# Last merge and output units of a two-block model on GpSimd's queue, five experts' units ahead of them, lower parts moved between sums

## The reference

```
h = rms_norm(x) * (1 + sc_m) + sh_m
proj = h @ w_in                                   # split into 9 parts, the last are 3 x 1024 gates
branches = [rglru(...), diff_attention(...), swa_attention(...)]
merged = sum_n sigmoid(gate_n) * (branch_n @ w_branch[n])      # 512 x 1024 each
x = x + g_m * (merged @ w_out)                                 # 1024 x 1024
h = rms_norm(x) * (1 + sc_f) + sh_f
top 4 of 32 experts per token by h @ w_router; softmax weights
x = x + g_f * sum over the four of  act(h @ w1[e] + b1[e]) @ w2[e] + b2[e]
```

## Time and profile before

| | |
|---|---|
| median of 3 runs | 2604.34 us (2603.31 to 2606.9) |
| profiled execution | 2605.9 us |
| its span in the trace | 2604.0 us |
| TensorE busy | 2567.9 us (99% of the span) |
| VectorE, ScalarE, GpSimd busy | 1350.1, 783.2, 73.6 us |
| TensorE's granted clock | 1.00 in every window used here |
| moved by DMA | 705.42 MB |

### The profile page before, as it was taken

The page is one execution under the profiler, slowest core; times in us unless marked ns, Lnnn a source line. Parts: engine busy times, 40 slices in busy tenths (PEclk is TensorE's granted clock), DMA queues, the critical chain, the costliest instruction groups (busy, mean ns, idle before and its releaser), DMA issues.

```text
span 2604.0 us, 39752 instructions
## 1 busy us (share of the span) xinstructions
PE 2567.9 (99%) x16005; PEld 1896.9 (73%) x16005; DVE 1350.1 (52%) x1781; ACT 783.2 (30%) x1318; POOL 73.6 (3%) x95
## 2 busy tenths in 40 slices
PE   9999999999999999999999999999999999999998
PEld 9989898999999899999999988833333333333333
DVE  6866785687688668657863684312112122112112
ACT  4414441443244144423433363122121121121111
POOL 0010200000000110000001000000000000000000
PEclk9999999999999999999999999999999999999999
DMA  6685443456655853344563634899999999999999
GB/s 231 212 287 178 139 146 146 151 179 227 219 180 184 303 172 125 135 146 162 178 219 109 230 125 175 322 416 426 427 427 427 428 427 427 427 427 428 427 428 411
DMA packets 265644, 705.42 MB, mean 271 GB/s; under 512 B 13108, under 2 KB 155392, under 8 KB 215744
## 3 DMA queue, kind: packets, MB, share of 16 engines
q1 hardware_dynamic: 253504, 663.66, 66.2%
q0 software_dynamic: 9856, 36.41, 3.9%
q10 hardware_dynamic: 2176, 3.83, 0.5%
HBM read 699.61 MB, written 6.60 MB: 271 GB/s over the span
## 4 chain that ended last, share of the span: by engine, by line
PE 79%; DMA 8%; SPq 8%; DVE 2%; ACT 1%; issue 1%; DVEq 0%; ACTq 0%; POOLq 0%
PE acc L1922 11%; PE acc L1124 6%; PE mix L1128 6%; PE acc L1126 6%; PE acc L1937 5%; PE acc L1197 5%; SPq L951 4%; PE mix L1118 3%; SPq L954 3%; PE acc L1070 3%; PE acc L1096 2%; PE acc L1147 2%; PE acc L1664 2%; PE acc L1456 2%; DMA area<-in_w 2%; PE acc L1213 2%
## 5 line engine op out<-in xcount | busy, mean ns | idle before, releaser
L1124 PE MATMUL acc<-branch_parts,area_parts 128*128 128x256 f32 x1176 | 343.8, 292 | 0.3 <-DVE big_parts L2580 0.2
L1128 PE MATMUL mix<-big_parts,zz_parts 128*128 128x256 f32 x1176 | 332.8, 283 | 0.0
L1126 PE MATMUL acc<-area_parts,ring_parts 128*128 128x256 f32 x1176 | 332.3, 283 | 0.0
L2580 DVE TENSOR_TENSOR ring_parts<-ring,area_parts 128x1792 fp32r<-128x1792 f32 (+2 forms) x139 | 262.5, 1888 | 93.1 <-ACT area_parts L2082 61.9
L3444 DVE COPY zz<-acc 128x512 f32<-128x512 f32 x32 | 22.1, 692 | 545.4 <-PE acc L1922 545.4
L1124 PEld LDWEIGHTS acc<-branch_parts,area_parts 128*128 128x128 f32 x1176 | 225.0, 191 | 9.6 <-DVE big_parts L2580 1.1
L1126 PEld LDWEIGHTS acc<-area_parts,ring_parts 128*128 128x128 f32 x1176 | 225.0, 191 | 0.2
L1128 PEld LDWEIGHTS mix<-big_parts,zz_parts 128*128 128x128 f32 x1176 | 224.9, 191 | 0.0
L2082 ACT ACTIVATE area_parts<-ring 128x1792 fp32r<-128x1792 f32 (+1 forms) x116 | 189.4, 1633 | 17.3 <-DMA ring<-in_ffn_up 12.8
L2673 DVE SCALAR_TENSOR_TENSOR zz_parts<-area_parts,ring_parts 128x1792 fp32r<-128x1792 f32 x84 | 170.1, 2025 | 6.3
L2074 ACT ACTIVATE area<-acc 128x512 f32<-128x512 f32 (+2 forms) x67 | 32.0, 478 | 346.9 <-PE acc L1857 334.7
(11 more groups left out here) (580 smaller groups left out, 4928.3 us busy)
## 6 DMA issues: line engine op xcount, KB each, us to landing
ring<-in_ffn_up SPq DMA_DIRECT2D x86, 1024.0 KB, 5.0
big<-in_w SPq DMA_DIRECT2D x79, 1024.0 KB, 25.4
ring<-in_w SPq DMA_DIRECT2D x76, 1024.0 KB, 25.8
ring<-in_w_in SPq DMA_DIRECT2D x72, 1024.0 KB, 7.0
area<-in_w SPq DMA_DIRECT2D x57, 1024.0 KB, 25.9
spare<-in_w SPq DMA_DIRECT2D x38, 1024.0 KB, 25.6
area<-in_w_ada POOLq DMA_DIRECT2D x24, 1024.0 KB, 8.6
ring<-in_ffn_down SPq DMA_DIRECT2D x28, 768.0 KB, 4.9
```

What stands on the lines that cost most here:

```text
L1124: pe.matmul(abank(a, b)[:, ts], wg[:, b, k, c * P:c * P + P], xg[:, k, :], start=c == 0 and k == 0, stop=False, skip_group_check=True)
L1126: pe.matmul(abank(a, b)[:, ts], wl[:, k, c0:c0 + P], xl[:, k, :], start=False, stop=k == K - 1, skip_group_check=True)
L1128: mm = pe.matmul(kbank(a, b)[:, ts], wk[:, b, k, c * P:c * P + P], xk[:, k, :], start=False, stop=k == K - 1, skip_group_check=True)
L2580: return v.tensor_tensor(out, a, b, op)
```

## The change

There are two edits that have nothing to do with each other.

The third merge unit and both output units are no longer issued by SyncE but by GpSimd, in halves, each after the same count of finished banks as before, and each half counts on one of four semaphores that have other uses earlier (`late_landed`). In GpSimd's queue they stand behind the bias blocks and ahead of `b1`, `b2` and `wr`. SyncE is thereby free of their waits: units 18 and 19 go straight after unit 2; unit 3 goes when group `G_MERGE2 + 1` is copied out, 12 and 13 when the second attention's output is copied out, then 4 and 5 as their groups are copied out, then 6 and 14 to 16.

In the split output stages ScalarE makes the upper part of unit 3 after the squares of group 0, not before them, together with that of unit 4. VectorE makes the lower part of unit 3 after the first ada half step of group 1, not before it.

```diff
+        late_landed = (((scr_a, 32), (scr_b, 16)), ((lru_landed, 256), (bias_landed, 32)))
...
         def half_landed(eng, L, r, hf, i=0):

             n = turn_of(L, r)
+            if L == LAYERS and r >= MERGE2 + 2:
+                s, before = late_landed[hf][r % 2]
+                eng.wait_ge(s, before + 16 * ((r - MERGE2) // 2))
+                return
...
-            for n in range(3):
+            for n in range(2):
                 r = MERGE2 + n
-                banks(L, 2 * ((last_group2(10), last_group2(11), G_MERGE2 + 1)[n] + 1))
+                banks(L, 2 * (last_group2(10 + n) + 1))
...
-                if n == 1:
-                    sp.wait_ge(z0_read, 1)
-                    first_units(0, 2, 3)
-            for n in range(2):
-                r = WOUT2 + n
-                banks(L, 2 * (G_MERGE2 + 4 + 2 * n))
-                plain(w_out2, WOUT2 + n, slice(UC * n, UC * n + UC))
+            sp.wait_ge(z0_read, 1)
+            first_units(0, 2, 3)
...
                 sp.wait_ge(w_used, q * UNITS_Q + 1)
+                first_units(q, 18, 20)
                 for n, a2 in ((3, G_MERGE2 + 1), (4, G_MERGE2 + 3), (5, G_MERGE2 + 5)):

                     sp.wait_ge(acc_free[a2 % 2], L * (GROUPS // 2) + a2 // 2 + 2)
                     first_units(q, n, n + 1)
+                    if n == 3:
+                        after(sp, pvs_out)
+                        first_units(q, 12, 14)
                 sp.wait_ge(merged_ready, 4 * LAYERS + 4)
                 first_units(q, 6, 7)
-                first_units(q, 18, 20)
-                first_units(q, 12, 17)
+                first_units(q, 14, 17)
...
                     if n != 1 and m % 2 == 0:
-                        for u in ((0, 1, 2, 3), (4,), (5,))[m // 2]:
+                        for u in ((0, 1, 2), (3, 4), (5,))[m // 2]:
                             down_upper(L, n // 2, u)
...
-                    if g == 1:
-                        down_lower(L, s, 3)
                     for at, j in enumerate(ada):
                         ada_half(8 * ADA_STAGES.index((L, a0)) + j)
-                        if at == 0 and g == 2:
-                            down_lower(L, s, 5)
+                        if at == 0 and g:
+                            down_lower(L, s, 2 * g + 1)
                         if at == (1 if g else 0) and g < 2:
                             down_lower(L, s, 2 * g + 2)
                     if not len(ada):
-                        for u in ((2,), (4,), (5,))[g]:
+                        for u in ((2,), (3, 4), (5,))[g]:
                             down_lower(L, s, u)
...
+            for a2, r in ((G_MERGE2 + 2, MERGE2 + 2), (G_MERGE2 + 4, WOUT2), (G_MERGE2 + 6, WOUT2 + 1)):
+                g.wait_ge(acc_done, LAYERS * (2 * GROUPS) + (2 * GROUPS + 2 * a2))
+                v = view(LAYERS, r).rearrange("p (k c) -> p k c", k=4 if r < WOUT2 else DC)
+                src = w_br2[:, 4 * ORDER2[2]:4 * ORDER2[2] + 4, :] if r < WOUT2 else w_out2[:, :, UC * (r - WOUT2):UC * (r - WOUT2) + UC]
+                h = 2 if r < WOUT2 else 4
+                for hf in range(2):
+                    g.dma_start(v[:, h * hf:h * hf + h, :], src[:, h * hf:h * hf + h, :]).then_inc(late_landed[hf][r % 2][0], 16)
+
             g.wait_ge(merged_ready, 4 * LAYERS + 4)
```

More of the change, by code:

```diff
@@ L583, in mixed_blocks @@
             ((small_landed, LAYERS * 176), (apart_landed, LAYERS * 48 + 16), (down_landed, LAYERS * 64), (const_landed, 112),
-             (rows_moved, 32), (landed[0], (LAYERS * (RINGED // 2) + 9) * 16)) + \
+             (rows_moved, 32), (landed[0], (LAYERS * (RINGED // 2) + 7) * 16)) + \
             tuple((w, 0) for w in w_landed_late)
@@ L3601, in _ @@
                     .then_inc(bias_landed, 16)
+            w_br2 = io["w_branch_2"].rearrange("l n (k p) c -> p (l n k) c", p=P)
+            w_out2 = io["w_out_2"].rearrange("l (k p) c -> p (l k) c", p=P)
+            for a2, r in ((G_MERGE2 + 2, MERGE2 + 2), (G_MERGE2 + 4, WOUT2), (G_MERGE2 + 6, WOUT2 + 1)):
[5 more added lines that the diff above has]
+                    g.dma_start(v[:, h * hf:h * hf + h, :], src[:, h * hf:h * hf + h, :]).then_inc(late_landed[hf][r % 2][0], 16)
             g.wait_ge(merged_ready, 4 * LAYERS + 4)
```

## The result

The changed kernel takes 2610.4 us (median of 14 executions, 2605.62 to 2623.38) against 2605.8 us for the kernel before, run beside it (14 executions). The ratio is 1.0021, with a 95% interval of 1.0012 to 1.0029: slower by 0.2%, where 2600.0 was forecast and the range ended at 2606.5. One execution is left out of them, a slow one of lower_stage1's twelve (5650.45 us). The profiled execution has a span of 2610.1 us, 6.1 more than the 2604.0 of before.

The account below looks back on a forecast made before the run. The end was taken as the start of the experts' unbroken DMA stream, set by TensorE's first buffer release, plus fixed bytes. Terms 0, 0 and -4.4 gave 2601.5 profiled, 2600.0 as median; range 2597.0 to 2606.5.

Parts of the forecast that it names:

- Units ahead: Expert units 18, 19, 3, 12, 13 and 4 issued earlier on SyncE: 0 us taken, at most 1.9.
- the dry engines: DMA engines idle about 1 us before the 21st expert unit, which waits for TensorE's first buffer release.
- Merge unit and first output unit on GpSimd: Before the output product: both loads stay hidden on GpSimd's queue, 0 us.
- The fixed count of bytes behind the 21st unit: Experts' stage: the kernel ends a fixed number of bytes after the unbroken load stream starts.
- Second output unit and router's weights: Router product at 1663.71: weights ready 0.5 us in time behind 2.10 MB on GpSimd; 0 taken, bounds 0 to 8.1.
- the nearest row: GpSimd's 1.05 MB DMA at the 8.6 us median: share 0.44, router's weights landing at 1662.7.
- the rule on turns by whole packets: DMA engines alternate queues by packet: GpSimd share 0.34, router's weights at about 1667, TensorE waiting some 4 us.
- my bound: All SyncE units up to 8 and 9 go first: router's weights land at 1671.3, TensorE waits 8.1 us.
- rival (b): Router's weights late at the router product: 4.0 us wait, 2604, chance 0.18; hard case 2610, chance 0.12.
- Part 2: Reordered lower parts in two ada output stages: 4.4 us gain, 2.9 first and 1.5 second, bounds 0 to 6.8.
- lower 4 ends at 663.4 as before: First ada stage: VectorE's lower part 4 keeps its end time, so the third ada step starts there, 2.9 us earlier.

Follow-up runs that it names:

- lower_stage1: Kernel before with VectorE's new order of lower parts in the first ada stage only, ScalarE's new order in both; ratio 0.9986.
- early_old_order: router_early with the old order of lower and upper parts, so only load places differ from the kernel before; ratio 1.0000 to the kernel before.
- out2_sync: Changed kernel with only the second output unit back on SyncE's queue, ahead of unit 5; ratio 0.9993 to the kernel before.
- router_early: Changed kernel with b1, b2 and the router's weights issued on GpSimd right behind the last merge unit; ratio 0.9985 to the kernel before.
- loads_only: Changed kernel with the old order of lower and upper parts, keeping the moved loads and units ahead; ratio 1.0039 to the kernel before.
- lower_only: Kernel before with only the new order of lower and upper parts, all loads where they were; ratio 0.9992.
- router_act: Changed kernel with b1, b2 and the router's weights issued by ScalarE at the same condition instead of GpSimd; ratio 1.0037 to the kernel before.
- early_held: router_early with units 18, 19, 3, 12, 13 and 4 held back behind the second output unit's condition; ratio 1.0007 to the kernel before.
- fill_short: Changed kernel with 10 calls of extra 256-column products on TensorE ahead of the first router product; ratio 1.0000 to the kernel before.

## Why the prediction was wrong, step by step

**Units ahead, 0: right.** early_old_order shows it against the kernel before, with the dry engines that were forecast ahead of the 21st unit.

**Merge unit and first output unit on GpSimd, 0: right** (out2_sync). The fixed count of bytes behind the 21st unit held too: 907.5 to 909.1 us in all fourteen profiles.

**Second output unit and router's weights, 0: this is the step that failed.** I took the share of 0.44 from the nearest row, GpSimd's ada loads, and set aside the rule on turns by whole packets because that row did not fit it. The rule's share of 0.34 was nearly right: measured 0.32 (2.62 of 8.23 MB). The ada loads' time to landing was a poor test of it: the rule speaks of two backlogged queues, and I had not looked at whether both were so there (no run here settles that). From the output unit's issue to the landing of the router's weights I had reckoned 16.9 us (1645.8 to 1662.7), by the rule 21.5 (to 1667.3) and by my bound 25.5 (to 1671.3); it took 22.7 (1643.55 to 1666.25). The two waits and what goes with them cost 5.6 us, inside the bounds of 0 and 8.1. The Trainium skill states in "DMA: Bandwidth & Descriptors", section "Queues, rings and completion order", that a DMA engine takes turns by whole packets between the queues that it has work for. The runs agree where both queues are backlogged (720 and 765 packets; 870 and 889; 632 and 594).

**The clock, not in the sum at all: 3.4 us.** Every rival with a wait priced it at its own length. A wait of 4.5 us took 3.4 more, and rival (b), priced at 4.0 us, came out at 5.6 + 3.4. Without the 3.4 the kernel would have stood at the edge of the range, 2607.0 against 2606.5. The Trainium skill, "TensorE: Matmul & The Clock Gate", section "Part 1: The HAM clock gate (the "warmup" mystery)", says that the array falls to 1.2 GHz when it has been idle; the trace agrees (0.50 from 1664 on), and I had not asked what it would make of a wait at this place.

The kernel before shows such a fall already, so "1.00 in every window used here" was true only of the windows that I had looked at. Behind the wait of 3.63 us the first product takes 0.58 us, and behind the 3.19 us in the other stage 0.39. The windows of the kernel before:

```profile
678.00:680.00 2.00, 1.41 (x6) 1.42 (x7) 1.85 (x4) 0.00 (x0) 0.16 (x1) 0.64 0.83 127
680.00:682.00 2.00, 2.00 (x12) 2.00 (x11) 1.33 (x2) 0.00 (x0) 0.00 (x0) 0.51 1.00 406
```

That is some 1.7 us of work lost (0.36 and 0.49 of 2 us each), a price that could have been read before the change. A wait doesn't always bring it. In the same stages the clock falls behind waits of 2.03 (router_early), 2.40 (changed) and 2.91 us (early_old_order), and not behind 3.19 (before) and 3.59 us (loads_only). What decides it, no run here shows.

**Part 2, 4.4 us (2.9 and 1.5): mechanism seen where the weights come in time, term too large.** The changed kernel's profile shows 2.5. In the first stage it goes as forecast there (third ada step at 663.87, one wait, 0.83, though before unit 3 and not before the last); in the second it waits 0.48 and 2.40 us, where 0.8 and 0.9 were foretold, and the clock falls behind the 2.40. The other profiles scatter widely. In router_early the first stage goes as forecast within 0.3 us: VectorE's third ada step starts at 663.15 (663.4 foretold). Over all profiles but lower_stage1's, waits for lower parts are 6.8, 6.2 and 5.8 us with the old order (mean 6.3), and with the new one in both stages 0.3 to 5.8 in ten (mean 3.2). The gain is 3.1 us, and the output product starts at 1642.1 on average instead of 1645.2. The stages gain alike, 1.5 us in the first (3.0 to 1.55; forecast 2.9) and 1.6 in the second (3.2 to 1.6; forecast 1.5). In the first the term that was mis-sized is "lower 4 ends at 663.4 as before". It needs ScalarE's upper part, and that the down unit's load. ScalarE in lower_only and in router_early:

```profile
662.70 1.06 ACT L2105 ACTIVATE area_parts<-ring 128x1024 fp32r<-128x1024 f32 x1 [11.77 <-DMA ring<-in_ffn_down]
```

```profile
659.60 1.06 ACT L2108 ACTIVATE area_parts<-ring 128x1024 fp32r<-128x1024 f32 x1 [8.36 <-DMA ring<-in_ffn_down]
```

Where it starts at 659.6 there is no wait for lower parts in this stage, where it starts at 662.7 there are 3.2 us. With the old order it starts at 658.8 to 659.8 (three profiles), with the new one at 658.5 to 662.8 (eleven profiles, with lower_stage1), over 661 in five of them. The ada load that the reorder brings forward, from 657.62 to 654.38, now stands beside the down unit. The queues of 652 to 662 us, of the kernel before and of lower_only:

```profile
q0 software_dynamic: 390, 1.47, 47.5%
q1 hardware_dynamic: 1471, 1.47, 43.9%
```

```profile
q0 software_dynamic: 595, 2.24, 64.1%
q1 hardware_dynamic: 1157, 1.17, 34.0%
```

GpSimd carries more and SyncE less in the new order. That this is what delays the down unit fits, but is argued from these rows, not shown by an experiment; nor is it known why it strikes in some executions only.

The terms together give the miss of the profiled execution, 2612.0 against 2601.5: 5.6 for the router's weights, 3.4 for the clock and 1.9 for part 2, less 0.5 behind the 21st unit.

## What to carry to other kernels

Before a load is moved to another queue, count packets, not bytes: where both queues were backlogged here they took turns by packets, so small packets beside large ones crawl, and a small load that something waits for should be issued early rather than on a queue of its own. Price a new wait on TensorE at more than its length, as the clock may fall with it (here 3.4 us on 5.6, and 1.7 on the wait of 3.63 that the kernel before had). Here issuing the router's weights some 35 us sooner, or holding three units back by one group, turned a loss of 0.2% into a gain of 0.15%, within noise the gain of part 2 alone.

## What the runs showed of the hardware that was not expected

**A second fall of the clock.** In the routing step, where TensorE has pauses of 0.2 us between short products in every profile, the clock falls in some executions and not in others. TensorE's 16 products of 256 columns, first in out2_sync, then in the changed kernel:

```profile
1688.54 3.43 PE L1884 MATMUL acc<-zz,area 128*64 128x256 f32 x16
```

```profile
1696.34 1.95 PE L1876 MATMUL acc<-zz,area 128*64 128x256 f32 x16
```

The window 1690 to 1692 of out2_sync has a granted clock of 0.50. It costs 1.2 to 1.7 us in router_act, out2_sync, early_held, fill_short and lower_stage1, and is absent from the other nine profiles. What decides it stays open.

**One queue, two packet sizes.** The same three loads are 176 packets on GpSimd's queue and 1232 on ScalarE's. Behind the output unit GpSimd's queue needs 720 packets in all for them, ScalarE's with nothing ahead 1232, which fits that the latter was slower (25.4 us against 20.1). No run changes the packet size on ScalarE's queue alone, and three queues share the engines there instead of two, so how much is due to which is not shown.
